# Retention with rows centred by TensorE, and the next stage's weights split during it

## What is computed

```
scores = (q @ k.T) * decay ;  o = scores @ v + (q @ S) * q_dec
S      = S * gamma**128 + (k * k_dec).T @ v
ro     = (o - mean(o)) * rsqrt(var(o) + eps) * gn_w        # over the 64 of a head
a      = concat(fo, ro) * silu(g)                          # fo: output of the attention
```

## Time and profile before

| | |
|---|---|
| median of 3 runs | 4133.45 us (4122.27 to 4133.8) |
| profiled execution | 4131.24 us, its span 4129.6 us |
| TensorE busy | 3565.7 us, 86% of the span |
| VectorE, ScalarE busy | 1694.8 us (41%), 1380.3 us (33%) |
| GpSimd busy | 371.6 us (9%) |
| mean granted TensorE clock | 0.924 of full speed |

### The profile page before, as it was taken

The page is one execution under the profiler, slowest core; times in us unless marked ns, Lnnn a source line. Parts: engine busy times, 40 slices in busy tenths (PEclk is TensorE's granted clock), DMA queues, the critical chain, the costliest instruction groups (busy, mean ns, idle before and its releaser), DMA issues. The chain is left out here.

```text
span 4129.6 us, 65450 instructions
## 1 busy us (share of the span) xinstructions
PE 3565.7 (86%) x21028; PEld 2654.2 (64%) x21028; DVE 1694.8 (41%) x3182; ACT 1380.3 (33%) x2379; POOL 371.6 (9%) x630
## 2 busy tenths in 40 slices
PE   6999799946899899899999675899968949959998
PEld 5888688833455555555555453688856737748887
DVE  3222311143345445444444376433334645643333
ACT  3111200012233333333333254433335656642222
POOL 0000000010122222122223111000000000000000
PEclk9999899957799999999999786899988979979999
DMA  4233522255577777777775455433334233252221
GB/s 150 103 129 121 167 93 100 91 116 167 166 241 232 215 235 231 216 229 232 236 231 176 134 193 185 167 127 112 115 132 156 82 125 106 90 172 87 85 79 61
DMA packets 376166, 628.11 MB, mean 152 GB/s; under 512 B 125209, under 2 KB 175041, under 8 KB 375874
## 3 DMA queue, kind: packets, MB, share of 16 engines
q1 hardware_dynamic: 334098, 488.34, 36.3%
q0 software_dynamic: 41792, 136.48, 10.5%
HBM read 489.46 MB, written 135.22 MB: 151 GB/s over the span
## 5 line engine op out<-in xcount | busy, mean ns | idle before, releaser
L1549 PEld LDWEIGHTS att_samp_ps_t<-att_ident,att_samp_k_ring 128*128 128x128 f32 x2048 | 237.4, 146 | 281.5 <-issue 231.0
L1549 PE MATMUL att_samp_ps_t<-att_ident,att_samp_k_ring 128*128 128x128 f32 x2048 | 338.0, 290 | 84.5 <-DVE att_samp_kt L1354 44.6
L123 PE MATMUL in_ps_z<-in_w_hi,in_u_hi 128*128 128x512 f32 x952 | 375.7, 395 | 36.4 <-DVE in_w_lo L156 36.4
L124 PE MATMUL in_ps_z<-in_w_lo,in_u_hi 128*128 128x512 f32 x952 | 374.4, 393 | 0.0
L125 PE MATMUL in_ps_z<-in_w_hi,in_u_lo 128*128 128x512 f32 x952 | 374.3, 393 | 0.0
L1149 POOL DMA_DIRECT2D att_samp_v_ring<-cache_v x512 | 274.8, 537 | 984.5 <-issue 982.1
L1239 ACT COPY att_samp_kt<-att_samp_ps_t 128x512 f32<-128x512 f32 x256 | 149.8, 585 | 501.3 <-PE att_samp_ps_t L1549 500.6
L1354 DVE COPY att_samp_kt<-att_samp_ps_t 128x512 f32<-128x512 f32 x256 | 176.2, 688 | 292.4 <-PE att_samp_ps_t L1549 287.8
L1503 PE MATMUL att_fox_ps_o<-att_fox_prob,att_fox_v_one 128*65 128x512 f32 (+3 forms) x640 | 286.9, 532 | 3.8 <-ACT att_fox_prob L1208 3.8
L1303 DVE TENSOR_REDUCE att_fox_part_max<-att_fox_ps_n 128x1 f32<-128x512 f32 (+2 forms) x320 | 195.1, 610 | 131.1 <-PE att_fox_ps_n L1470 115.1
L1208 ACT ACTIVATE att_fox_prob<-att_fox_ps_k 128x512 f32<-128x512 f32 (+1 forms) x320 | 169.9, 536 | 189.5 <-DVE att_fox_ps_k L1322 110.5
(11 more groups left out here) (365 smaller groups left out, 6898.3 us busy)
## 6 DMA issues: line engine op xcount, KB each, us to landing
att_samp_v_ring<-cache_v POOLq DMA_DIRECT2D x512, 256.0 KB, 3.8
att_samp_k_ring<-cache_k SPq DMA_DIRECT2D x512, 256.0 KB, 3.5
tail_a_hi<-a_hi SPq DMA_DIRECT2D x34, 512.0 KB, 5.6
tail_a_lo<-a_lo SPq DMA_DIRECT2D x34, 512.0 KB, 5.9
in_w_stage<-w_in_even SPq DMA_DIRECT2D x64, 256.0 KB, 6.4
lru_u_hi<-u_hi SPq DMA_DIRECT2D x8, 2048.0 KB, 8.0
lru_u_lo<-u_lo SPq DMA_DIRECT2D x8, 2048.0 KB, 13.2
in_x<-x SPq DMA_DIRECT2D x17, 512.0 KB, 3.9
```

The costliest lines, as they stand in the source:

```text
L123: pe.matmul(out, act_hi, w_hi, start=start, stop=False)
L124: pe.matmul(out, act_hi, w_lo, start=False, stop=False)
L1549: last = pe.transpose(ps_t[:, a * PAGE:(a + 1) * PAGE], k_ring[:, n % 2, p, a * P:(a + 1) * P], ident[:, :])
```

## The change

In `retention`: the tile loops are written out; q, k and v have three buffers instead of two; `q_decayed` and `gated` have two. The rows are centred by TensorE: `turn_rows` multiplies the kept output with a constant matrix (the identity less 1/64 within a head) instead of transposing it, and writes over `ps_o`. VectorE's `centre` is gone for prompt tiles (the sample tile is centred once, ahead of the loop); the square (ScalarE) and `normed` (VectorE) read the centred rows from PSUM. The state's decay and the attention half of the gated rows go to GpSimd. The factor 0.5 of the gates moves into the evacuation of the stage that makes them (`tensor_copy` becomes `tensor_scalar`, and a scale of ScalarE). One more constant is loaded. TensorE's, ScalarE's and VectorE's orders change.

The 20 pieces of `ple_proj` and `w_out` of the first tail are loaded and split during retention, two in each of the steps 0 to 9, through two staging buffers: SyncE loads at the head of a step, ScalarE makes the rounded half at the end of its step, GpSimd the rest at the end of its own. The first tail then loads and splits the 16 pieces of `ple_gate_w` alone, with four buffers. The second tail is as before.

```diff
+def retention(nc, io, held):
     with ExitStack() as ctx:
         ph = Phase(nc, ctx, "ret")
         PAIRS = H // 2
+        QB = 3
...
+        ps_r = ps_o[:, :, :].rearrange("p a (n e) -> p (a n) e", n=2)
...
+        def two(t):
+            n = len(held.pieces)
+            return min(2 * t, n), min(2 * t + 2, n)
+        def centred_rows(t):
+            return ps_r if prompt(t) else cen[:, :, :]
...
+            fetch_qkv(0)
+            fetch_gate(0)
             sp.dma_start(ro_new[:, :, :].rearrange("p h e -> p (h e)"), io["ro"]).then_inc(new_in, 16)
-            sp.wait_ge(*u_done.at(0))
-            fetch_qkv(2, 0)
-            def step(t, i, par):
+            fetch_qkv(1)
+            fetch_gate(1)
+            fetch_qkv(2)
+            for t in range(T):
+                held.load(sp, *two(t))
                 if prompt(t + 3):
-                    sp.wait_ge(*u_done.at(t + 1))
-                    fetch_qkv(t + 3, 1 - par)
-                if not static(t + 2, LAST):
-                    sp.wait_ge(*gated_rows.at(t))
-                    fetch_gate(t + 2, par)
+                    sp.wait_ge(*u_done.at(t))
+                    fetch_qkv(t + 3)
+                if t + 2 <= LAST:
+                    sp.wait_ge(*fox_gated.at(t))
+                    fetch_gate(t + 2)
                 sp.wait_ge(*a_low.at(t))
                 sp.dma_start(row(io["a_hi"], t), a_hi[:, :].bitcast(F32)).then_inc(a_stored, 16)
                 sp.dma_start(row(io["a_lo"], t), a_lo[:, :].bitcast(F32)).then_inc(a_stored, 16)
...
+            def scale_state(t):
+                flat = state[:, :, :, :].rearrange("p a n e -> p (a n e)")
+                pool.wait_ge(*o_done.at(t))
+                pool.wait_ge(*added.at(t - 1))
+                pool.tensor_tensor(flat, flat, g_tab[:, :], ALU.mult).then_inc(scaled.sem, 1)
+            def weigh_gates(t):
                 pool.wait_ge(*silu_made.at(t))
                 pool.wait_ge(*gated_rows.at(t - 1))
                 pool.tensor_tensor(silu_gn[:, :], silu[:, W:], gn[:, :], ALU.mult).then_inc(silu_weighted.sem, 1)
-            decay_k(0, 0, 0)
-            each_tile(pool, step)
+                pool.wait_ge(gate_in[t % 2], 48 * (t // 2 + 1))
+                pool.wait_ge(*a_turned.at(t - 2))
+                pool.tensor_tensor(gated[:, t % 2, 0:W], fo[:, t % 2, :], silu[:, 0:W], ALU.mult).then_inc(fox_gated.sem, 1)
+            for t in range(-1, LAST):
+                if prompt(t + 1):
+                    decay_k(t + 1)
+                    scale_state(t + 1)
+                weigh_gates(t + 1)
+                held.make_low(pool, *two(t + 1))
...
+            def square(t):
+                if prompt(t):
+                    act.wait_ge(*r_turned.at(t))
+                else:
+                    act.wait_ge(centred, 1)
                 act.wait_ge(*var_sum.at(t - 1))
-                act.activation(sq[:, :, :], cen[:, :, :], ACT.Square).then_inc(squared.sem, 1)
-                if prompt(t + 1):
-                    keep_o(t + 1)
+                act.activation(sq[:, :, :], centred_rows(t), ACT.Square).then_inc(squared.sem, 1)
+            def step(t):
                 act.wait_ge(*var_made.at(t))
                 act.activation(var[:, 2, :], var[:, 1, :], ACT.Sqrt).then_inc(rooted.sem, 1)
                 if prompt(t + 2):
-                    place(t + 2, i + 1, par)
-                if not static(t + 1, LAST):
-                    tanh_gate(t + 1, i + par, 1 - par)
+                    place(t + 2)
+                if t < LAST:
+                    tanh_gate(t + 1)
+                if prompt(t + 1):
+                    keep_o(t + 1)
                 act.wait_ge(*a_turned.at(t))
                 act.wait_ge(a_stored, 32 * (t + 1))
                 act.copy(a_hi[:, :], ps_a[:, :]).then_inc(a_high.sem, 1)
-            place(0, 0, 0)
+                if t < LAST:
+                    square(t + 1)
+                held.make_high(act, *two(t))
+            place(0)
+            tanh_gate(0)
             keep_o(0)
-            tanh_gate(0, 0, 0)
-            place(1, 0, 1)
-            each_tile(act, step)
+            square(0)
+            place(1)
+            for t in range(T):
+                step(t)
...
+            def add_update(t):
                 dve.wait_ge(*scaled.at(t))
                 dve.wait_ge(*u_done.at(t))
                 for half in range(2):
                     last = dve.tensor_tensor(state[rows, :, half, :], state[rows, :, half, :], ps_u[rows, :, half, :], ALU.add)
                 last.then_inc(added.sem, 1)
...
+            def step(t):
                 dve.wait_ge(*squared.at(t))
                 dve.tensor_reduce(var[:, 0, :], sq[:, :, :], AX.X, ALU.add).then_inc(var_sum.sem, 1)
                 dve.wait_ge(*var_sum.at(t))
                 dve.tensor_scalar(var[:, 1, :], var[:, 0, :], 1.0 / HD, EPS, ALU.mult, ALU.add).then_inc(var_made.sem, 1)
-                if prompt(t + 1):
-                    update(t + 1)
                 dve.wait_ge(*rooted.at(t))
                 dve.reciprocal(var[:, 3, :], var[:, 2, :]).then_inc(inverted.sem, 1)
                 dve.wait_ge(*inverted.at(t))
-                dve.tensor_tensor(normed[:, :, :], cen[:, :, :], var[:, 3, :].unsqueeze(2).broadcast_to([P, H, HD]), ALU.mult)\
+                dve.tensor_tensor(normed[:, :, :], centred_rows(t), var[:, 3, :].unsqueeze(2).broadcast_to([P, H, HD]), ALU.mult)\
                     .then_inc(normed_rows.sem, 1)
                 dve.wait_ge(*normed_rows.at(t))
                 dve.wait_ge(*silu_weighted.at(t))
-                dve.tensor_tensor(gated[:, W:], normed[:, :, :].rearrange("p h e -> p (h e)"), silu_gn[:, :], ALU.mult).then_inc(gated_rows.sem, 1)
-                if not static(t + 1, LAST):
-                    gate_silu(t + 1, i + par, 1 - par)
+                dve.wait_ge(*a_turned.at(t - 2))
+                dve.tensor_tensor(gated[:, t % 2, W:], normed[:, :, :].rearrange("p h e -> p (h e)"), silu_gn[:, :], ALU.mult)\
+                    .then_inc(gated_rows.sem, 1)
                 if prompt(t + 2):
                     decay_q(t + 2)
-                    decay_scores(t + 2)
+                if t < LAST:
+                    gate_silu(t + 1)
+                if prompt(t + 1):
+                    add_update(t + 1)
                 dve.wait_ge(*a_high.at(t))
                 dve.tensor_tensor(a_lo[:, :], ps_a[:, :], a_hi[:, :].bitcast(F32), ALU.subtract).then_inc(a_low.sem, 1)
-                if not static(t + 1, LAST):
-                    centre(t + 1, i + par, 1 - par)
+                if prompt(t + 2):
+                    decay_scores(t + 2)
             decay_q(0)
             decay_scores(0)
-            update(0)
-            gate_silu(0, 0, 0)
-            centre(0, 0, 0)
+            centre_new()
+            gate_silu(0)
             decay_q(1)
+            add_update(0)
             decay_scores(1)
-            each_tile(dve, step)
+            for t in range(T):
+                step(t)
...
+                pe.wait_ge(*normed_rows.at(t - 1))
                 for a in range(PAIRS):
-                    pe.matmul(ps_o[:, a, :], state[:, a].rearrange("p n e -> p (n e)"), q_dec[:, a, :], start=True, stop=False,
+                    pe.matmul(ps_o[:, a, :], state[:, a].rearrange("p n e -> p (n e)"), q_dec[:, t % 2, a, :], start=a == 0, stop=False,
                               skip_group_check=True)
+                for a in range(PAIRS):
                     for half in range(2):
                         h = 2 * a + half
-                        last = pe.matmul(ps_o[half * HD:(half + 1) * HD, a, :], qkv[:, par, 2, h * HD:(h + 1) * HD], sc[:, h, :],
+                        last = pe.matmul(ps_o[half * HD:(half + 1) * HD, a, :], qkv[:, t % QB, 2, h * HD:(h + 1) * HD], sc[:, h, :],
                                          start=False, stop=half == 1, skip_group_check=True)
                 last.then_inc(o_done.sem, 1)
...
             def turn_rows(t):
                 pe.wait_ge(*o_kept.at(t))
-                pe.wait_ge(*added.at(t))
                 for a in range(PAIRS):
-                    last = pe.transpose(ps_u[:, a].rearrange("p n e -> p (n e)"), o_t[:, a, :], ident[:, :])
+                    last = pe.matmul(ps_o[:, a, :], o_t[:, a, :], centre[:, :], start=True, stop=True)
                 last.then_inc(r_turned.sem, 1)
...
+            for t in range(T):
+                if prompt(t + 2):
+                    turn_qk(t + 2)
                 if prompt(t + 1):
-                    attend(t + 1, 1 - par)
-                if prompt(t + 2):
-                    turn_qk(t + 2, i + 1, par)
+                    attend(t + 1)
+                turn_gated(t)
                 if prompt(t + 1):
-                    add_to_state(t + 1, 1 - par)
                     turn_rows(t + 1)
+                    add_to_state(t + 1)
                 if prompt(t + 2):
                     score(t + 2)
-                turn_gated(t)
...
+class TailWeights:
```

(85 more changed lines are left out.)

170 lines of the change are left out of this document (77 added, 93 removed).

## The result

The changed kernel takes 4142.45 us (median of 8 runs, 4134.89 to 4145.39); the kernel before, run beside it, 4131.70 (8 runs). The ratio is 1.0029, 95% interval 1.0017 to 1.0041: slower by 10.7 us. The forecast was slower by 25 us. The profiled execution took 4134.89 us, 7.6 less than its own median; its first attend begins 5.9 us earlier than in the trace of before. So the places are compared by distances within the trace, not by the two totals.

The account below looks back on a forecast made before the run. Retention was taken as bound by a chain from engine to engine, with no engine full. Steps with pieces +54, without -7, start +2.5, end -8, tail -16: +25, 4156 us; 8-in-10 range 4122 to 4192.

Parts of the forecast that it names:

- The mechanism: In retention, two low halves delay GpSimd's decay_k, so TensorE stands still 5.2 us ahead of add_to_state.
- Rival 2: In retention, the split is hidden and all 14 intervals take 11.9 us: -47, 4084 us; chance 0.06.
- the step with two pieces: Retention's ten intervals from attend 1 to attend 11: 19.1 us each instead of 13.68, +54 us.
- the middle, 19.1 us: Step with pieces, taken between 16.35 us at full clock and 21.9 at half clock.
- The base step: Retention's step before the change, taken as the mean over all steps, 13.68 us between attends.
- the last four: Retention's intervals without pieces, attend 11 to 15: 1.8 us less each, -7 us.
- The start: Attend 0 to attend 1: from 15.7 to about 17.8 us, with one more constant loaded; +2.5 us together.
- End: Attend 15 to the last a_lo: from 29.4 to 21 or 22 us, -8 us.
- tail: First tail: the first gate product moves from 2615 to about 2599, -16 us.
- The loads: Staged pieces in retention land in time for ScalarE, by a thin margin of 4 us.
- A step without pieces: Retention: 8.0 us between attends, attend 3.15 less 0.5; 10.65 at full clock, 11.9 with some 20% at half.
- the regrouping: Attend with state products first: gains between 0 and 0.8 us, taken as 0.5 (1.0 at half clock).

Follow-up runs that it names:

- experiment 1: The changed kernel with GpSimd's low halves made one step later, behind the next tile's decay_k, scale_state and gates: 4090.11 us (0.9895), again 4087.64 us (0.9902).
- experiment 7: The new retention without weight pieces, its attend interleaved as in the kernel before: 4140.11 us, ratio 1.0028.
- experiment 8: The kernel before with only its attend regrouped, eight state products first and then sixteen with the scores: 4113.71 us, ratio 0.9965.
- experiment 4: The kernel before, its retention order kept and loops written out, with the weight pieces staged and split in retention: 4106.88 us, ratio 0.9938.
- experiment 2: The changed kernel without weight pieces in retention, the first tail loading and splitting all 36 itself: 4096.94 us, ratio 0.9915.

## Why the prediction was right or wrong

**The mechanism was right.** The two low halves lie between two neighbours of TensorE's list, TensorE waits 5 us ten times, and experiment 1, which moves only the low halves, gives 52 us. Rival 2, the hidden split, was priced at 4084; with the split hidden the kernel takes 4088 to 4090.

**The size was off**, +25 against +9 in the trace. The failed step is the one with two pieces: "I take the middle, 19.1 us" between the ends of 16.35 and 21.9. It was 18.06 on average, which makes 10.4 us of the 16 missing. The reason for the middle was that what follows a long pause runs at half clock; that held for what came right behind the pause (`add_to_state` in all ten steps, part or all of the scores), but in seven of the ten not for the attend and the turnings, which ran at full clock again. The mean clock in the ten steps was 0.85, against 0.87 in the same ten before: ten standstills of 5 us cost hardly any of it. The rule of the Trainium skill's "TensorE: Matmul & The Clock Gate", Part 1, taken alone for 21.9, was further off than the middle.

**The smaller terms.** The base step was 13.52 us in the first ten intervals, not the mean of 13.68 (1.6 us the other way), and 14.1 in the last four, so those gave 9.3 instead of 7. The start was 4.8 us better than forecast: it started from the 15.7 us of before, much of it at half clock, and here the groups behind the first attend ran at full clock (the row below). This distance scatters by 2 us: it is 11.7 and 13.6 us in the two traces of experiment 1's kernel. End (8) and tail (16, measured 18) were right. The loads were in time: ScalarE never waits for a staged piece in retention.

```profile
2323.23 1.09 PE L1948 MATMUL ret_ps_q<-ret_ident,ret_qkv 128*128 128x128 f32 x8
```

**A step that came out right for the wrong reason.** A step without pieces was forecast at 11.9 and took 11.76. It was built from 8.0 us between attends and an attend 0.5 us shorter, with a fifth at half clock. Measured at full clock, it is 11.0: 8.9 and 2.1. The gap was 0.9 too short (`turn_rows` waits for ScalarE's copy, and VectorE's update and `a_lo` stand ahead of the scores), the attend 0.5 too long. Worse, the regrouping was priced as a small saving of its own, between 0 and 0.8 us, and the rest of the 1.8 us a step was credited to the new order. Experiments 7 and 8 show that neither has a single price. The new order costs 0.3% with the interleaved attend and gains 0.5% with the grouped one (0.9915 against 0.9965); the regrouping gains 0.35% in the old order and 1.1% in the new one (0.9915 against 1.0028), where five groups of TensorE stand in a row and the mean clock rises from 0.73 to 0.85 with it. Without that edit the change stands at 4184 us, where the prediction's own working, with half a microsecond more in each of 14 steps, would have said about 4163. So it is luck that the forecast came as near as it did: it used half clock where the runs show full, and missed most of what the regrouping was worth.

**The tail.** What the pieces were staged for is real: 18 us, seen in the changed kernel and in experiment 4.

## What to carry to other kernels

When background work is put into a stage bound by a chain between engines, ask what stands behind it in the list of the engine that does it, and what it waits for itself: the same work fed from the step before cost 1 us a step instead of 6. Sort small products so that those with the same weight shape stand together, above all where TensorE's groups follow each other on the path; the pauses are short, but the clock that went with them about doubled their price here. And try a cheap edit both with and without the large one beside it before crediting a gain to either.

## What was not expected of the hardware

- A change between 128x128 and 128x64 weights costs TensorE 0.17 us at full clock (the mean of six) and 0.22 to 0.33 at half.
- The granted clock was lower with the attend interleaved: 0.73, against 0.85 with it grouped (experiments 7 and 2, from attend 1 to attend 15). In the old order it was 0.84 and 0.90. A standstill of 5 us in each step did not lower it like that: the changed kernel held 0.85 in its ten steps with pieces, experiment 1 without the standstill 0.82. Why the clock follows the short pauses is not shown by any run.
- GpSimd holds up VectorE: 0.17 us became 1.24 next to the low halves. The silu of 1.23 us lasted 2.12 in one step of the changed kernel, at no cost, since VectorE was idle for 1.67 us behind it. The Trainium skill, "SBUF — State Buffer", SBUF: two separate sides, has the two engines share a pair of ports that one of them holds for its whole instruction. The rows agree: the mean ends when GpSimd's low halves do, and the silu 1.1 us after GpSimd's instruction, about its own length.

```profile
2539.14 1.27 POOL L1783 TENSOR_TENSOR ret_state<-ret_state,ret_state_table 128x512 f32<-128x512 f32 x1 [5.23 <-PE ret_ps_o L1972]
...
2539.38 2.12 DVE L1898 SCALAR_TENSOR_TENSOR ret_silu<-ret_tanh,ret_gate 128x1024 f32<-128x1024 f32 x1 [1.71 <-ACT ret_tanh L1822]
```
